# Output projection of a two-layer encoder: two groups of VectorE work put in another order

## The reference, cut to what matters

```python
for layer in range(DEPTH):                     # DEPTH = 2, x is 1024 x 1024 fp32
    h = rms_norm(x, norm_g[layer])
    z = h @ w_in[layer]                        # attention and retention branches, gates
    ...
    merged = gates[:, :, 0] * ya + gates[:, :, 1] * yb
    x = x + merged @ w_out[layer]              # the output projection, where the change lies
return rms_norm(x, final_norm_g)
```

## Time and profile before

| | |
|---|---|
| median of 3 runs | 1846.5 us (1844.35 to 1846.97) |
| the profiled execution, its own time | 1846.6 us |
| its span | 1844.8 us |
| mean granted TensorE clock | 0.991 |
| busy share | PE 95%, VectorE 68%, ScalarE 43%, GpSimd 40% |

### The profile page before, as it was taken

How to read it: one execution, slowest core, us unless ns; L and a number is a source line. 1 busy time by engine, 2 the same in 40 slices (tenths; PEclk the granted TensorE clock), 3 DMA queues, 4 the chain that set the end, 5 groups by cost and what they waited for, 6 DMA issues and landing times.

```text
span 1844.8 us, 29679 instructions
## 1 busy us (share of the span) xinstructions
PE 1754.7 (95%) x10592; PEld 1552.7 (84%) x10592; DVE 1249.5 (68%) x2494; ACT 800.5 (43%) x1791; POOL 729.2 (40%) x646
## 2 busy tenths in 40 slices
PE   6999999999999999999899998999999999999986
PEld 6887878899999888887697888889999998888865
DVE  7789569625534387769986976694345544867798
ACT  5488448622123243334354873683222223433333
POOL 2267438624333323233623764484223322232240
PEclk9999999999999999999999999999999999999998
DMA  7000000111011322233130001001011023222322
GB/s 270 24 12 13 27 23 24 39 32 47 23 34 43 132 67 92 87 102 143 46 118 24 24 17 35 12 13 47 24 46 45 29 86 115 73 76 86 132 80 92
DMA packets 133784, 113.07 MB, mean 61 GB/s; under 512 B 13600, under 2 KB 112672, under 8 KB 133664
## 3 DMA queue, kind: packets, MB, share of 16 engines
q1 hardware_dynamic: 131264, 106.20, 17.9%
q10 hardware_dynamic: 2400, 5.31, 0.8%
HBM read 90.52 MB, written 20.97 MB: 60 GB/s over the span
## 4 chain that ended last, share of the span: by engine, by line
PE 68%; DVE 16%; ACT 4%; issue 3%; DMA 0%; POOL 0%; DVEq 0%; SPq 0%; ACTq 0%; POOLq 0%
PE ps L768 16%; PE ps L770 16%; PE ps L769 16%; PE ps L906 4%; PE ps L895 3%; PE ps L919 3%; PE ps L921 2%; DVE xh L2168 2%; PE ps L1012 2%; PE ps L996 1%; DVE hT_lo L2155 1%; DVE pT_lo L1799 1%; DVE lsum L2146 1%; DVE us L1900 1%; DVE nmx L1791 1%
## 5 line engine op out<-in xcount | busy, mean ns | idle before, releaser
L768 PE MATMUL ps<-w_hi,hT_hi 128*128 128x256 f32 (+1 forms) x1280 | 390.7, 305 | 6.7 <-DVE w_lo L1666 4.8
L770 PE MATMUL ps<-w_hi,hT_lo 128*128 128x256 f32 (+1 forms) x1280 | 376.1, 294 | 0.0
L769 PE MATMUL ps<-w_lo,hT_hi 128*128 128x256 f32 (+1 forms) x1280 | 375.7, 294 | 0.0
L768 PEld LDWEIGHTS ps<-w_hi,hT_hi 128*128 128x128 f32 x1280 | 244.3, 191 | 11.4 <-DVE w_lo L1666 5.2
L769 PEld LDWEIGHTS ps<-w_lo,hT_hi 128*128 128x128 f32 x1280 | 244.6, 191 | 0.3
L770 PEld LDWEIGHTS ps<-w_hi,hT_lo 128*128 128x128 f32 x1280 | 244.1, 191 | 0.0
L622 POOL TENSOR_SCALAR pp<-pp,rrc 128x1024 f32<-128x1024 f32 x128 | 144.2, 1126 | 149.0 <-DVE rrc L1804 149.0
L1799 DVE TENSOR_TENSOR pT_lo<-ps,pT_hi 128x512 fp32r<-128x512 f32 x256 | 164.2, 682 | 24.2 <-ACT pT_hi L1316 23.0
L906 PE MATMUL ps<-idf,pp 128*128 128x128 f32 x1024 | 141.6, 278 | 18.2 <-DVE pT_lo L1799 12.3
L1316 ACT CAST pT_hi<-ps 128x512 fp32r<-128x512 f32 x256 | 138.4, 590 | 43.6 <-PE ps L906 42.0
L1791 DVE TENSOR_REDUCE nmx<-ps 128x1 f32<-128x1024 f32 x128 | 154.4, 1206 | 2.6 <-PE ps L895 2.6
(11 more groups left out here) (217 smaller groups left out, 4089.5 us busy)
## 6 DMA issues: line engine op xcount, KB each, us to landing
raw<-w_in SPq DMA_DIRECT2D x167, 256.0 KB, 3.3
xs<-xh SPq DMA_DIRECT2D x2, 4096.0 KB, 14.3
ys<-y_st SPq DMA_DIRECT2D x32, 256.0 KB, 2.1
hb<-ys SPq DMA_DIRECT2D x16, 512.0 KB, 4.3
xh<-xs SPq DMA_DIRECT2D x8, 1024.0 KB, 7.5
raw<-w_a SPq DMA_DIRECT2D x16, 256.0 KB, 3.1
raw<-w_r SPq DMA_DIRECT2D x16, 256.0 KB, 3.2
w<-w_o SPq DMA_DIRECT2D x4, 1024.0 KB, 6.2
```

The costliest lines, as they stand in the source:

```text
L768: nc.tensor.matmul(outp, ah, bh, start=(start and i == 0), stop=False)
L769: nc.tensor.matmul(outp, ah, bl, start=False, stop=False)
L770: last = nc.tensor.matmul(outp, al, bh, start=False, stop=(stop and i == len(pairs) - 1))
```

## The change

Two edits. In VectorE's queue `add_up(0)` is cut in two halves of row tiles, each ahead of one half of `right_lo(2)`; and `right_lo(4)` and `right_lo(5)` go in front of `left_sum(5)` and `left_lo(5)`, with `add_up(2)` between the two right ones. In ScalarE's queue `left_hi(5)` goes behind `right_hi(4)` and `right_hi(5)`. No instruction is added or removed on any engine but the waits at the head of the second half of `add_up(0)`.

```diff
                 left_hi(4)
-                left_hi(5)
                 right_hi(4)
                 right_hi(5)
+                left_hi(5)
                 left_hi(6)
...
-                def add_up(p):
+                def add_up(p, rows=range(4)):
...
-                    for i in range(4):
+                    for i in rows:
...
                 left_sum(3)
-                add_up(0)
-                right_lo(2)
+                for h in range(2):
+                    add_up(0, (2 * h, 2 * h + 1))
+                    right_lo(2, (h,))
                 left_lo(3)
                 add_up(1)
                 right_lo(3)
                 left_lo(4)
+                right_lo(4)
+                add_up(2)
+                right_lo(5)
                 left_sum(5)
-                add_up(2)
                 left_lo(5)
-                right_lo(4)
-                right_lo(5)
                 add_up(3)
```

## The result

| | before | after |
|---|---|---|
| median of 7 runs each | 1846.27 us (1843.31 to 1846.97) | 1851.88 us (1851.17 to 1853.38) |
| ratio, 95% interval | | 1.0036 (1.0025 to 1.0048): slower |
| span of the profiled execution | 1844.8 us | 1849.6 us |
| layer 0, first `left_sum(1)` to `add_up(5)` | 71.8 us | 75.6 us |
| layer 1, first `left_sum(1)` to the last norm | 87.1 us | 89.5 us |

Together they grew by 3.8 + 2.4 = 6.2 us. The rest of the span, which no edit touches, lies between 1684.3 and 1686.8 us in the eleven profiles (1685.9 before, 1684.5 after), so profiles are compared by these stretches, one profile for each kernel. Executions of one kernel spread by 1.5 to 7 us.

A forecast was written before the change was run, and what follows sets the result against it. The prediction took VectorE to bound the output projection stage, never resting. Layer 1's +2.45 us and layer 0's +2.2 us made 4.65 us, so 1846.5 + 4.7 = 1851.2 us, in a range of 1845.5 to 1854.5.

The forecast's parts named there:

- VectorE bounds the stage: Output projection: VectorE is busy 62.42 of 62.42 us in layer 1 and never rests, so its instructions set the time.
- Rival C: TensorE's waits are what the stage is paid in: 3.7 us a layer won, 1839.1 us in all; chance 0.06.
- `add_up(0)` in halves costs nothing and gives nothing: VectorE's queue: cost 0 to 0.1 us, taken as 0; TensorE's 1.15 us wait ahead of product 2 goes without gain.
- `right_sum(6)` comes forward and VectorE waits for one of its instructions, 2.4 us: Released early by `right_lo(4)`, its second instruction falls among two-SBUF-input pairs: 2.2 + 0.2 us, bounds 0 and 4.5.
- Rival B: VectorE goes first all along, `right_sum(6)`'s second instruction slips to `add_up(3)`: +0.5 to +1.5 us, 1847.5 us; chance 0.25.
- rival D: Both of GpSimd's instructions are waited for: 4.5 us a layer, 1855.5 us in all; chance 0.07.
- The inputs of `right_lo(4)` are ready: In `left_sum(5)`'s old place at 1786.22, `right_lo(4)` finds its high part made at 1784.1, ready by 2 us: cost 0.
- `left_sum(5)` ahead of `left_lo(5)` costs 0.05 us: With nothing between them the cast must fit; `left_sum(6)` and `left_lo(6)` already stand so and lose 0.05 us.
- Layer 0, +2.2 us: Layer 0's tail: next layer's loads go out 6.7 us sooner, moving weight slices; +2.2 us, bounds +1.3 and +4.6.
- The sum: Layer 1's 2.45 us plus layer 0's 2.2 us: 4.65 us, giving 1851.2 us, 0.25% slower.
- The signs: What the changed profile would show, such as a pair of about 4.5 us at `right_lo(5)` or just behind.
- TensorE's gap of about 3 us ahead of product 6: Sign in TensorE's timeline: after product 5 it waits about 3 us for `right_lo(6)`, which comes 2.45 us later.

The follow-up runs named there:

- `right_sum(6)` held: The changed kernel, with `right_sum(6)` on GpSimd also waiting for `left_lo(5)`: median 1847.28 us, ratio 1.0006 to the kernel before.
- first edit alone: The kernel before with only `add_up(0)` in halves between the halves of `right_lo(2)`: median 1846.39 us against 1844.91, ratio 1.000.
- the turn fixed: The changed kernel, with the second instruction of `right_sum(4)` waiting for the first half of `right_lo(3)`: median 1850.89 us, ratio 1.0024 to the kernel before.
- second edit alone: The kernel before with `right_lo(4)`, `add_up(2)`, `right_lo(5)` ahead of `left_sum(5)` and `left_lo(5)`, ScalarE's queue to match: median 1852.72 us, ratio 1.0035.
- two sums under `add_up`: The kernel before with `add_up(0)` ahead of `left_sum(3)`, `add_up(1)` ahead of `left_lo(3)`, `right_hi(2)` ahead of `left_hi(3)`: median 1840.99 us against 1846.22, ratio 0.9971.
- the sums apart: As two sums under `add_up`, plus `right_sum(4)` waiting for `left_lo(4)` and `add_up(2)` ahead of `left_sum(5)`: median 1844.60 us, ratio 0.9995 to the kernel before.

## Why the prediction was right, point by point

- *VectorE bounds the stage.* Shown. It stayed busy without a gap, and with `right_sum(6)` held TensorE's gap ahead of product 4 was gone and the time was not shorter. Rival C falls.
- *`add_up(0)` in halves costs nothing and gives nothing.* Shown by the first edit alone (1.000).
- *`right_sum(6)` comes forward and VectorE waits for one of its instructions, 2.4 us.* Shown from both sides: the pair at 1793.35 took 4.56 us where it took 2.27, and holding the sum back gave 2.2 us in layer 1. The small term, up to 0.2 us for its first instruction, came to 0.1. Layer 1's stretch grew by 2.38 against a forecast of 2.45. Rival B falls in every profile of the changed order (five of them without the hold, ten stages), and rival D too: the pair takes 4.6 us in all ten, one instruction waited for.
- *The inputs of `right_lo(4)` are ready, and `left_sum(5)` ahead of `left_lo(5)` costs 0.05 us.* VectorE shows no gap at either; 2.34 us between the starts at 1797.91 and 1800.25, where an undisturbed pair takes 2.27.
- *Layer 0, +2.2 us.* The mechanism was right and the term was mis-sized, through one of its steps: "The third still waits for product 5, now over at 909.9", which is 62.1 us behind the stage's start. In the profile of the change product 5 ended 66.8 us behind it, because GpSimd had the turn at `right_lo(3)` and product 3 began late, so the third and fourth slices lay over all of `mean_square`: 6.76 us where 4.9 was forecast, and the stretch +3.8. With VectorE first (the turn fixed) the end was at 62.5 and the stretch +2.3, the parts being: the right sum +2.4, left parts of product 6 +1.6 (forecast +1.8), `right_lo(6)` 2.98 us against 2.92 (forecast 0.5 more), `mean_square` 5.65 us (forecast 4.9), the norm -0.4 (forecast -0.3). The misses at `right_lo(6)` and in `mean_square` nearly cancel, which was luck.
- *The sum.* 4.65 us were forecast; the medians differ by 5.6, the ratio makes it 6.6, the stretches 6.2. So the forecast was short by 1 to 2 us, and that its 1851.2 lies 0.7 us from the measured median is in part luck. The turn in layer 0 is worth 1.3 to 1.5 us of it when it goes to GpSimd.
- *The signs.* Seen as forecast: no idle time on VectorE, the slow pair at `right_lo(5)`, `right_sum(6)` 37.0 us behind the stage's start (forecast 1788.7, the same), the wait ahead of product 4 gone, layer 0's loads 43.8 us behind the start (forecast 44.0). Not seen: TensorE's gap of about 3 us ahead of product 6. With product 3 late its products ran on without one; with the second edit alone, where product 3 is not late, it is there in layer 1, 2.58 us.

## What to carry to other kernels

Here one engine bounds the stage, and the order of its queue moved nothing by itself; what moved the time is what another engine's instruction lay under. Before putting work forward, look at who is released by it: here `right_lo(4)` was put 7 us forward, a GpSimd sum that had lain for free under eight PSUM additions came forward with it and landed on a pair that cannot run beside it. Read the durations of equal instructions against each other; three slow pairs of 4.5 us a layer among those of 2.27 were there to be seen, and taking two of them away gave 0.33%.

## What the runs showed of the hardware

- The turn between VectorE and GpSimd is not settled by the program's order alone. At the end of `add_up(1)` it went to GpSimd (`right_sum(4)` 4.71 us) and to VectorE (5.79 us) in two layers of one execution, and it shifted product 3 by 2.2 us. GpSimd starts 0.02 to 0.03 us ahead of VectorE's went with GpSimd's turn in three layers; with 0.01 ahead to 0.02 behind it was VectorE's, in eleven. VectorE's own total was the same either way (pairs of 4.57 and 4.52 us).
- A GpSimd instruction that has been waiting since VectorE's first of two instructions mostly goes ahead of the second. The exception in the kernel before (1795.42) was seen again with the first edit alone and with two sums under `add_up`, but with the sums apart the same spacing went to GpSimd, in both layers, and in the kernel before itself it did so at the pair at 1770.21, which `right_sum(3)` met 0.23 us behind its start. What decides it was not found.
- Tiny VectorE instructions (128x4) suffer most for their length: a dozen took 2.37 us undisturbed and 5.2 to 7.2 us beside weight slices on GpSimd, so where slices lie relative to such a chain was worth about 1 us either way.
